# Splitting four products of a gate unit into high and low parts, and reordering vector work in an up-projection unit

## Chip, cores and metric

One core of a Trainium2 (trn2) chip runs the whole program. The metric is the device time of one execution in microseconds (us); the median of several runs counts.

## What is computed

One layer of a hybrid autoregressive decoder, for a prompt of 512 positions and 8 single-position samples that share the weights (520 columns in all), model width 2048, everything in fp32. The parts that matter here:

```python
def layer(x, ...):
    ...
    h2 = rmsnorm(x, g_ffn_pre)
    up, gt = jnp.split(h2 @ w_ffn_up, 2, axis=-1)          # 2048 -> 2 x 5632
    uc, new_ffn = causal_dwconv(up, prev_ffn, ffn_conv_w)
    f = (jax.nn.gelu(uc + ffn_conv_b, approximate=True) * gt) @ w_ffn_down
    x = x + rmsnorm(f, g_ffn_post)
    x = x + jax.nn.sigmoid(x @ w_ple_gate) * (p @ w_ple)   # w_ple_gate: 2048 -> 2048
```

The change lies in `h2 @ w_ffn_up` ("up") and in `x @ w_ple_gate` ("gate").

## The kernel before

**Units and products.** Each large matrix product is cut into units. A unit makes two tiles of 128 output features for all 520 positions. Operand and weights are seen as 2x2 blocks (upper and lower half of the contraction, left and right 260 columns), and a unit computes them by seven block products, numbered 0 to 6, in place of eight (a Strassen-Winograd scheme). For that it needs sums and differences of the operand blocks, made once for each set of units (`t1` to `t4`, lines 1947 to 1975), and of the weight blocks, made in each unit: `s1` (in these sets done by GpSimd's two DMAs, the second accumulating, lines 2573 to 2588), `s3` (L1921), `s2` (L1931) and `s4` (L1940). Product 1 reads the `s1` sum, product 2 the `s2` difference and `t2`, product 4 `s3` and `t3`, product 5 `s4`, product 6 `t4`. Every product has two halves of four contraction tiles each.

**Two ways to do a product.** A raw product (`raw_product`, L1023) multiplies fp32 tiles: 8 matmuls, which the profile shows as 16 records. A split product (`split_product`, L1058) takes a high and a low part of both factors and does three cheaper matmuls a tile, 24 in all: high x high, low x high, high x low. It needs the weight's high part `v_hi` (ScalarE, `v_high`, L1219), its low part `v_lo` (VectorE, `v_low`, L1889; four buffers for each, in turn), the operand's high part `o_hi` (ScalarE, `o_high`, L1246) and its low part `lo` (VectorE, `o_low`, L1987). The operand's parts are made once for a set, the weights' in each unit.

**Sets.** The seven sets of units (`SETS`) are: the input projection, w_o, up (set 2, 44 units, from `U_UP`), three for down, and gate (`S_GATE`, 8 units, from `U_GATE`). The first unit of sets 0, 2 and 6 is plain (`plain_unit`, L989): eight fp32 block products with no differences at all, since these are made meanwhile. The second unit of these three sets is done raw in all seven products (`in_fp32` says so); all later units are split. Sets 1, 3, 4 and 5 split products 0 to 4 of their second unit already (`early_split`).

**What sets the order.** Each engine runs its own list of instructions, in the order in which the program text emits it, and waits on semaphores. In gate, VectorE's list in `plain_unit` (L2056 to 2076) is `s3`, `t1`, `t2`, `t3`, `t4`, `o_low(0)`; then `second_unit` (L2078) emits slot by slot, for i from 0 to 13, evictions, `s2`, `s4`, `s3` of the next unit, the `o_low` that `lows` names, and `v_low`. In up it is `t1`, `s3`, `t2`, `t3`, `t4`, and in `second_unit` `s2` first, then `o_low` 0 to 4 in slots 1, 3, 5, 7, 9; `o_low(5)` comes at the unit's end and `o_low(6)` in slot 1 of the third unit. ScalarE's list in gate's `plain_unit` (L1289) is `o_high` 0 to 4 and then four copies out of PSUM (L1299); product 0 of the second unit waits for the first of these. `unit` (VectorE at L2106, ScalarE at L1322) is the list of an ordinary unit: `v_low` or `v_high` four halves ahead, slot by slot.

SyncE loads the weights (`load`), a quarter at a time, once the quarter's last reader is done; in gate its list between the second and the fourth unit also has the two stores of the first unit's output, and loads of `pl_sb` and `xx_sb`.

Of the kernel before, what the change touches and what calls it, by code (L numbers as in the profile page):

```python
# [26 lines left out]
U_UP = U_O + KD // 2  # L27
# [36 lines left out]
def h_of(u, j, h=0):  # L64
    return 14 * u + 2 * j + h + (2 * NBR if u >= U_O else 0) + (NPH if u >= U_UP else 0)
# [18 lines left out]
def build(nc, sstream, x_in, p_in, chan_in, sinkp_in, sinks_in, cstate_in, fstate_in,  # L84
# [5 lines left out]
    with ExitStack() as ctx:  # L90
# [173 lines left out]
        def set_of(u):  # L264

            return max(s for s, (u0, _, _) in enumerate(SETS) if u >= u0)

        def is_first(u):
            return u == SETS[set_of(u)][0]
# [8 lines left out]
        def is_second(u):  # L278
            return u > 0 and is_first(u - 1)
# [7 lines left out]
        def early_split(s):  # L287

            return s in (1, 3, 4, 5)

        def in_fp32(u, j):

            return is_first(u) or is_second(u) and (j >= 5 or not early_split(set_of(u)))

        def low_order(s):

            return (0, 3, 1, 5, 2, 4, 6) if s == S_GATE else (0, 1, 2, 3, 4, 5, 6)

        def summed(u):

# [21 lines left out]
        def s_of(u, j, h=0):  # L322
            return place[u, j, h]
# [36 lines left out]
        def of_form(s):  # L360

            return s if s < 3 else s - 3
# [811 lines left out]
        def _(act):  # L1174
# [114 lines left out]
            def plain_unit(s, d11, d12, d22, d21):  # L1289

                u = SETS[s][0]
                early = 1 if s == 2 else 5
                for j in range(early):
                    o_high(s, j)
                act.wait_ge(v_used, h_of(u, 6, 1) + 1)
                for dst, (a, b), done in ((d11, (0, 1), c11_out), (d12, (1, 1), c12_out),
                                          (d22, (1, 0), c22_out), (d21, (0, 0), c21_out)):
                    if dst is not None:
                        nc.scalar.activation(dst, pair[a][:, b, 0:HALF], ACT.Copy).then_inc(done, 1)  # L1299
                for j in range(early, 2 if s == 2 else 5):  # L1300
                    o_high(s, j)
# [20 lines left out]
            def unit(u, evac, ahead=14):  # L1322

                n = s_of(u, 0)
                for i in range(14):
                    if (u, i // 2, i % 2) in place and s_of(u, i // 2, i % 2) + 4 < n + ahead:
                        v_high(s_of(u, i // 2, i % 2) + 4)
                    evac(u, i)
                    if u == U_GATE + 2 and i == 2:
                        o_high(S_GATE, 6)  # L1330

            def by(s, evac, first=None, last=14):

                u0, n, _ = SETS[s]
                if early_split(s):
                    early_unit(s, first or evac)
                    unit(u0 + 1, evac, 18)
                else:
                    if u0 not in PLAIN:
                        first_unit(s, first or evac)  # L1340
                    second_unit(s, evac)
                for u in range(u0 + 2, u0 + n):
                    unit(u, evac, 16 if u == U_O - 1 else 18 if u == U_UP - 1 else 14 if u == u0 + n - 1 else 18)

# [309 lines left out]
        def _(dve):  # L1654
# [269 lines left out]
            def s2(u, h):  # L1924

                if u >= U_END:
                    return
                if in_fp32(u, 0):
                    dve.wait_ge(v_used, h_of(u, 0, h) + 1)
                sum_ready_1(dve, u, h)  # L1930
                dve.tensor_tensor(quarter(u, 0, h), w_src(u, 1, h), quarter(u, 0, h), ALU.subtract)\  # L1931
                   .then_inc(s2_done, 1)
# [44 lines left out]
            def o_low(s, j):  # L1977

                if s == S_GATE and j == 5:
                    slot_free(dve, s, 5)  # L1980
                for h in range(2):
                    if s < S_GATE or j not in (0, 3, 5):
                        u = SETS[s][0]
                        dve.wait_ge(v_used, h_of(u + 1 if in_fp32(u + 1, j) else u, j, h) + 1)
                    dve.wait_ge(o_hi_rdy, 14 * s + 2 * j + h + 1)
                    k = halves(s, h)
                    dve.tensor_tensor(lo_of(s, j)[:, k, :], raw_of(s, j)[:, k, :],  # L1987
                                      o_hi[j][:, k, :].bitcast(f32), ALU.subtract).then_inc(o_rdy, 1)

            def both_halves(f, *a):  # L1990
                f(*a, 0)
                f(*a, 1)
# [63 lines left out]
            def plain_unit(s):  # L2056

                u = SETS[s][0]
                if s == 2:
                    for k in range(KH):  # L2060
                        h2_row(k)
                    dve.wait_ge(h2_rdy, KH)
                    both_halves(t1, s)
                both_halves(s1, u + 1)
                both_halves(s3, u + 1)
                if s == 2:
                    for k in range(KH, KD):
                        h2_row(k)
                    dve.wait_ge(h2_rdy, KD)
                else:  # L2070
                    both_halves(t1, s)
                both_halves(t2, s)
                both_halves(t3, s)
                both_halves(t4, s)
                if s == S_GATE:
                    o_low(s, 0)

            def second_unit(s, evac):  # L2078

                u = SETS[s][0] + 1  # L2080
                nxt = s_of(u + 1, 0)
                lows = {1: 3, 3: 1, 4: 5, 5: 2, 9: 4} if s == S_GATE else {2 * j + 1: j for j in range(6)}
                if s == 2:
                    lows = {1: 0, 3: 1, 5: 2, 7: 3, 9: 4}
                for i in range(14):
                    if i < 13:
                        evac(u, i)
                    if i in (0, 1):
                        s2(u, i)
                    if i in (2, 3):  # L2090
                        s1(u + 1, i - 2)
                    if i in (6, 7):
                        s4(u, i - 6)
                    if i in (8, 9):
                        s3(u + 1, i - 8)
                    if i in lows:
                        o_low(s, lows[i])
                    if i >= 10:
                        v_low(nxt + i - 10)
                    if i in (11, 12):  # L2100
                        s2(u + 1, i - 11)
                evac(u, 13)
                if s == 2:
                    o_low(s, 5)

            def unit(u, evac, last):  # L2106

                n = s_of(u, 0)
                ahead = 16 if u == U_O - 1 else 14 if last and u != U_UP - 1 else 18
                adds = set_of(u) in (4, 5)  # L2110
                first = (1, 3, 5, 9) if adds else (9,)
                for i in range(14):
                    if i in first:
                        evac(u, i)
                    if (u, i // 2, i % 2) in place and s_of(u, i // 2, i % 2) + 4 < n + ahead:
                        v_low(s_of(u, i // 2, i % 2) + 4)
                    if is_second(u) and i == 1:
                        o_low(set_of(u), 4)
                    if is_second(u) and i == 13:
                        o_low(set_of(u), 5)  # L2120
                    if is_second(u - 1) and i == (5 if u > U_GATE else 1):
                        o_low(set_of(u), 6)
                    if i in (4, 5):
                        s4(u, i - 4)
                    if i in (8, 9) and u != U_O - 1 and u + 1 not in PLAIN:
                        s1(u + 1, i - 8)
                    if i in (10, 11) and u != U_O - 1 and u + 1 not in PLAIN:
                        s3(u + 1, i - 10)
                    if i in (12, 13) and not last:
                        s2(u + 1, i - 12)  # L2130
                    if i not in first:
                        evac(u, i)

            def by(s, evac, first=None):
                u0, n, _ = SETS[s]
                if early_split(s):
                    early_unit(s, first or evac)
                    unit(u0 + 1, evac, False)
                else:
                    if u0 in PLAIN:  # L2140
                        plain_unit(s)
                    else:
                        first_unit(s, first or evac)
                    second_unit(s, evac)
                for u in range(u0 + 2, u0 + n):
                    unit(u, evac, u == u0 + n - 1)

# [585 lines left out]
```

## Time and profile before

| | |
|---|---|
| median of 3 runs | 2707.23 us |
| lowest, highest | 2706.88, 2708.92 us |
| the profiled execution's own time | 2706.55 us |
| its span, first to last instruction | 2704.4 us |
| TensorE busy | 2683.6 us (99%) |
| VectorE busy | 2162.8 us (80%) |
| ScalarE busy | 1361.9 us (50%) |
| mean granted TensorE clock | 0.999 of 2.4 GHz |

The span is what the trace shows; 2.15 us of the execution lie around it. Busy shares are averages over stages, so the stretches of the two units have to be read by themselves. In a timeline a row is one instruction or several merged ones: start, time from first start to last end, engine, line, what it writes and reads, and in brackets the idle time of the engine before it with what ended it. TensorE names only the kernel's tiles: `pair` is PSUM. "issue" is a wait for which the profile shows no releaser.

### The profile page before, as it was taken

What the parts mean: (1) busy time and instruction counts of PE and PEld (TensorE: products, weight loads), DVE (VectorE), ACT (ScalarE), POOL (GpSimd) and SP (SyncE); (2) the same over time, 40 slices, a digit from 0 to 9 for tenths busy, and PEclk for the clock granted to TensorE, in tenths of its full rate; (3) what the DMA queues carried; (4) which work ended last, traced back from release to release, by engine and by line L of the source; (5) the groups of instructions that cost most, each with busy time, mean ns of one, the idle gap of its engine ahead of it and who ended that gap; (6) DMA issues with size and microseconds to landing.
All of it is one profiled execution on the core that took longest, in us unless ns stands there. A gap on an engine that the chain in (4) does not pass through costs nothing.

```text
span 2704.4 us, 55262 instructions
## 1 busy us (share of the span) xinstructions
PE 2683.6 (99%) x21029; PEld 2615.1 (97%) x21029; DVE 2162.8 (80%) x3845; ACT 1361.9 (50%) x2459; POOL 144.4 (5%) x214
## 2 busy tenths in 40 slices
PE   9999999999999999999999999999999999999999
PEld 8999999999999999979999999999999999999899
DVE  5988888777753587898888888888888768789887
ACT  5444455555542255645555555555555453445344
POOL 0000000000000000000000000000000000000000
PEclk9999999999999999999999999999999999999999
DMA  6333333333344455565566655666568575565674
GB/s 225 119 118 119 111 114 116 122 129 130 120 181 140 168 141 148 190 213 170 161 189 189 187 160 164 208 183 189 154 187 294 164 240 166 163 205 167 227 257 150
DMA packets 150356, 458.29 MB, mean 169 GB/s; under 512 B 15881, under 2 KB 46481, under 8 KB 146816
## 3 DMA queue, kind: packets, MB, share of 16 engines
q1 hardware_dynamic: 125184, 367.61, 38.1%
q0 software_dynamic: 24864, 88.52, 14.8%
q8 instruction: 81, 1.33, 0.2%
q14 instruction: 83, 0.68, 0.1%
q10 hardware_dynamic: 144, 0.15, 0.0%
HBM read 403.37 MB, written 54.11 MB: 169 GB/s over the span
## 4 chain that ended last, share of the span: by engine, by line
PE 97%; DVE 1%; issue 1%; ACT 0%; DMA 0%; SPq 0%; DVEq 0%; ACTq 0%
PE pair L1058 76%; PE pair L1023 7%; PE pair L1142 7%; PE pair L989 3%; PE pair L803 1%; PE pair L1112 1%; PE pair L871 1%; PE pair L894 1%; PE pair L885 1%; PE pair L819 0%; DVE v_lo L1889 0%; PE pair L955 0%; DMA s_raw<-in_sstream 0%; DVE nv_s L1676 0%; DVE lo L1987 0%
## 5 line engine op out<-in xcount | busy, mean ns | idle before, releaser
L1058 PE MATMUL pair<-o_hi,v_hi 128*128 128x260 f32 x5778 | 1639.5, 284 | 2.1 <-DVE v_lo L1889 1.9
L1058 PE MATMUL pair<-o_hi,v_lo 128*128 128x260 f32 x5778 | 1631.2, 282 | 0.0
L1219 ACT ACTIVATE v_hi<-s_raw 128x512 fp32r<-128x512 f32 (+1 forms) x1328 | 826.5, 626 | 1006.8 <-PE pair L1058 841.9
L1058 PE MATMUL pair<-lo,v_hi 128*128 128x260 f32 x4140 | 1170.2, 283 | 0.0
L1889 DVE TENSOR_TENSOR v_lo<-s_raw,v_hi 128x512 fp32r<-128x512 f32 (+1 forms) x1264 | 859.4, 682 | 341.6 <-ACT v_hi L1219 302.1
L1058 PEld LDWEIGHTS pair<-o_hi,v_hi 128*128 128x128 f32 x5778 | 1086.3, 188 | 15.8 <-issue 12.5
L1058 PEld LDWEIGHTS pair<-o_hi,v_lo 128*128 128x128 f32 x5778 | 1088.5, 188 | 0.0
L1058 PEld LDWEIGHTS pair<-lo,v_hi 128*128 128x128 f32 x4140 | 778.1, 188 | 0.4
L1058 PE MATMUL pair<-lo_E,v_hi 128*128 128x260 f32 x834 | 236.0, 283 | 0.0
L1058 PE MATMUL pair<-lo_A,v_hi 128*128 128x260 f32 x804 | 226.6, 282 | 0.0
L1219 ACT ACTIVATE v_hi<-s_one 128x512 fp32r<-128x512 f32 (+1 forms) x212 | 132.1, 626 | 178.2 <-PE pair L1058 153.3
L1931 DVE TENSOR_TENSOR s_raw<-s_one,s_raw 128x512 f32<-128x512 f32 (+1 forms) x226 | 151.9, 675 | 14.6 <-PE pair L1023 14.6
L1058 PEld LDWEIGHTS pair<-lo_E,v_hi 128*128 128x128 f32 x834 | 156.5, 188 | 0.1
L1940 DVE TENSOR_TENSOR s_raw<-s_raw,s_raw 128x512 f32<-128x512 f32 (+1 forms) x226 | 152.3, 675 | 0.0
L1921 DVE TENSOR_TENSOR s_raw<-s_raw,s_raw 128x512 f32<-128x512 f32 (+1 forms) x226 | 151.3, 675 | 0.0
L1058 PEld LDWEIGHTS pair<-lo_A,v_hi 128*128 128x128 f32 x804 | 151.1, 188 | 0.0
L1889 DVE TENSOR_TENSOR v_lo<-s_one,v_hi 128x512 fp32r<-128x512 f32 (+1 forms) x212 | 143.3, 678 | 5.2 <-ACT v_hi L1219 1.7
L1023 PE MATMUL pair<-raw,s_raw 128*128 128x260 f32 x628 | 141.1, 383 | 1.0 <-issue 0.5
L1023 PEld LDWEIGHTS pair<-raw,s_raw 128*128 128x128 f32 x628 | 118.5, 190 | 19.8 <-issue 0.9
L2586 POOL DMA_DIRECT2D s_one<-in_sstream x81 | 44.4, 548 | 1385.7 <-DVE s_raw L1931 1053.8
L1142 PE MATMUL pair<-br_hi,v_lo 128*128 128x260 f32 x512 | 103.2, 283 | 0.0
L1142 PE MATMUL pair<-br_lo,v_hi 128*128 128x260 f32 x512 | 103.0, 283 | 0.0
(229 smaller groups left out, 2358.6 us busy)
## 6 DMA issues: line engine op xcount, KB each, us to landing
s_raw<-in_sstream SPq DMA_DIRECT2D x468, 512.0 KB, 4.8
s_one<-in_sstream POOLq DMA_DIRECT2D x146, 512.0 KB, 5.2
raw<-f_scr SPq DMA_DIRECT2D x12, 1040.0 KB, 7.4
s_raw<-in_sstream SPq DMA_DIRECT2D x32, 384.0 KB, 4.0
g_scr<-d_h SPq DMA_DIRECT2D x16, 520.0 KB, 2.7
g_in<-g_scr SPq DMA_DIRECT2D x32, 260.0 KB, 2.7
x_scr<-y_sb SPq DMA_DIRECT2D x8, 1040.0 KB, 4.9
s_one<-in_sstream POOLq DMA_DIRECT2D x16, 384.0 KB, 4.7
```

Source lines behind the costliest of these rows:

```text
L803: mm = pe.matmul(pair[2 + n][:, h, 0:HALF], w[:, quarter_of(k)[2]], x_half(k, h), start=k == 0, stop=k == KD - 1, skip_group_check=True)
L871: mm = pe.matmul(bank[g][:, v * 256:(v + 1) * 256], q_blk[n % 2][HD * g:HD * g + HD, v, :], kT_sb[HD * g:HD * g + HD, blk * BLK:(blk + 2) ...
L989: mm = pe.matmul(pair[a][:, b, 0:HALF], s_raw[r % 2][q][:, k % KH * P:(k % KH + 1) * P], src, start=k == 0, stop=k == nk * 2 - 1, skip_gro ...
L1023: mm = pe.matmul(out, w[:, kk * P:kk * P + P], src[:, k, :], start=j in (0, 1, 3) and k == 0, stop=k == nk - 1, skip_group_check=True)
L1058: mm = pe.matmul(out, wt[:, slot, kk * P:kk * P + P], r[:, k, :], start=j in (0, 1, 3) and k == 0 and n == 0, stop=k == nk - 1 and n == 2, ...
L1142: mm = pe.matmul(pair[2 + p][:, half, 0:HALF], wt[:, slot, kk * P:kk * P + P], r[:, half * HALF:(half + 1) * HALF], start=k == 0 and i == ...
L1219: nc.scalar.activation(v_hi[:, n % 4, 0:width], src, ACT.Copy, scale=0.5 if u == "br" else 1.0).then_inc(v_hi_rdy, 1)
L1889: ins = dve.tensor_tensor(v_lo[:, n % 4, 0:width], src, high, ALU.subtract)
L1921: dve.tensor_tensor(quarter(u, 2, h), quarter(u, 0, h), quarter(u, 2, h), ALU.subtract)\
L1931: dve.tensor_tensor(quarter(u, 0, h), w_src(u, 1, h), quarter(u, 0, h), ALU.subtract)\
L1940: dve.tensor_tensor(quarter(u, 1, h), quarter(u, 1, h), quarter(u, 0, h), ALU.subtract)\
L2586: pool.dma_start(s_one[:, 0:n], sstream[r_of(u), 2, :, 0:n]).then_inc(s1_dma, 16)
```

## The change

Gate's second unit computes products 0 to 3 split and 4 to 6 raw. For it ScalarE makes four `v_hi` ahead of the four copies, and VectorE's list gets behind `t4`: `o_low(0)`, two `v_low`, `o_low(1)`, two `v_low`, `s2` of the second unit, `o_low(2)`, `o_low(3)`; the unit itself runs through the ordinary `unit`, with `o_low(5)` in slot 1 and `o_low(4)` in slot 11. In up, `s2` of the second unit is emitted ahead of `t3` and `t4`, `t4` behind `o_low(0)`, and `o_low` 5 and 6 in slots 2 and 5 of the third unit.

```diff
+        def first_raw(s):
+            return 4 if s == S_GATE else 5 if early_split(s) else 0
         def in_fp32(u, j):
-            return is_first(u) or is_second(u) and (j >= 5 or not early_split(set_of(u)))
+            return is_first(u) or is_second(u) and (j >= first_raw(set_of(u)))
         def low_order(s):
-            return (0, 3, 1, 5, 2, 4, 6) if s == S_GATE else (0, 1, 2, 3, 4, 5, 6)
+            return (0, 1, 2, 3, 5, 4, 6) if s == S_GATE else (0, 1, 2, 3, 4, 5, 6)
...
@@ scalar, plain_unit
                     o_high(s, j)
+                if s == S_GATE:
+                    for n in range(4):
+                        v_high(s_of(u + 1, 0) + n)
                 act.wait_ge(v_used, h_of(u, 6, 1) + 1)
...
@@ scalar, unit
                     evac(u, i)
+                    if u == U_GATE + 1 and i == 1:
+                        o_high(S_GATE, 5)
...
@@ scalar and vector, by
-                    second_unit(s, evac)
+                    if s == S_GATE:
+                        unit(u0 + 1, evac, ...)
+                    else:
+                        second_unit(s, evac)
...
@@ vector, o_low
-                    if s < S_GATE or j not in (0, 3, 5):
+                    if s == S_GATE and j in (1, 2):
+                        dve.wait_ge(t4_done, 2 * of_form(s) + 2)
+                    elif s < S_GATE or j not in (0, 3, 5):
...
@@ vector, plain_unit
                 both_halves(t2, s)
-                both_halves(t3, s)
-                both_halves(t4, s)
+                if s != 2:
+                    both_halves(t3, s)
+                    both_halves(t4, s)
                 if s == S_GATE:
+                    nxt = s_of(u + 1, 0)
                     o_low(s, 0)
+                    v_low(nxt)
+                    v_low(nxt + 1)
+                    o_low(s, 1)
+                    v_low(nxt + 2)
+                    v_low(nxt + 3)
+                    both_halves(s2, u + 1)
+                    o_low(s, 2)
+                    o_low(s, 3)
...
@@ vector, second_unit
-                    if i in (0, 1):
+                    if i in (0, 1) and s != 2:
                         s2(u, i)
+                    if i == 0 and s == 2:
+                        both_halves(s2, u)
+                        both_halves(t3, s)
+                    if i == 2 and s == 2:
+                        both_halves(t4, s)
...
                 evac(u, 13)
-                if s == 2:
-                    o_low(s, 5)
...
@@ vector, unit
                     if is_second(u) and i == 1:
-                        o_low(set_of(u), 4)
-                    if is_second(u) and i == 13:
-                        o_low(set_of(u), 5)
-                    if is_second(u - 1) and i == (5 if u > U_GATE else 1):
+                        o_low(set_of(u), 5 if u > U_GATE else 4)
+                    if is_second(u) and i == (11 if u > U_GATE else 13):
+                        o_low(set_of(u), 4 if u > U_GATE else 5)
+                    if u == U_UP + 2 and i in (2, 5):
+                        o_low(2, 5 + i // 5)
+                    elif is_second(u - 1) and u != U_UP + 2 and i == (5 if u > U_GATE else 1):
                         o_low(set_of(u), 6)
```

## Rows read from the trace of the kernel before

**Rows 1.** The page's first part: busy time, share of the span, instructions.

```profile
PE 2683.6 (99%) x21029; PEld 2615.1 (97%) x21029; DVE 2162.8 (80%) x3845; ACT 1361.9 (50%) x2459; POOL 144.4 (5%) x214
```

**Rows 2.** TensorE's waits: releaser, total us, times, longest.

```profile
PE pair L1023 <- issue: 6.1, 3, 4.3
PE pair L1058 <- DVE v_lo L1889: 1.9, 3, 1.2
```

**Rows 3.** Chain of waits, in order of time: start, us, what; up, then gate.

```profile
1181.28 4.30 issue
1185.58 19.46 PE pair L1023 x80
...
2523.14 28.29 PE pair L989 x128
2551.44 1.26 issue
2552.69 24.79 PE pair L1023 x112
2577.48 121.03 PE pair L1058 x1008
```

**Rows 4.** TensorE's timeline in up: second unit, then products 2 and 3 of the third.

```profile
1177.61 3.67 PE L1023 MATMUL pair<-raw,s_one 128*128 128x260 f32 x16
1185.58 5.43 PE L1023 MATMUL pair<-raw_E,s_raw 128*128 128x260 f32 x16 [4.30 <-issue]
...
1211.38 0.39 PE L1058 MATMUL pair<-o_hi,v_hi 128*128 128x260 f32 x1 [0.49 <-DVE v_lo L1889]
...
1215.76 0.39 PE L1058 MATMUL pair<-o_hi,v_hi 128*128 128x260 f32 x1 [1.24 <-DVE v_lo L1889]
```

**Rows 5.** Windows: stretch, length, TensorE busy, granted clock, DMA share, GB/s.

```profile
1185.60:1188.00 2.40, 2.40 (x8) 0.66 0.12 22
1188.00:1190.00 2.00, 2.00 (x7) 0.55 0.72 244
...
2553.00:2556.00 3.00, 3.00 (x15) 1.00 0.80 321
```

**Rows 6.** VectorE's timeline in up, second and third unit.

```profile
1177.88 2.39 DVE L1959 TENSOR_TENSOR raw_E<-raw 128x1040 f32<-128x1040 f32 x2
...
1184.80 1.29 DVE L1931 TENSOR_TENSOR s_raw<-s_one,s_raw 128x512 f32<-128x512 f32 x2
...
1190.61 0.69 DVE L2460 TENSOR_TENSOR fzb<-fzb,rstd 128x520 f32<-128x520 f32 x1
...
1193.53 0.69 DVE L1940 TENSOR_TENSOR s_raw<-s_raw,s_raw 128x512 f32<-128x512 f32 x1
...
1199.73 0.42 DVE L2157 TENSOR_TENSOR g_half<-pair,g_half 128x260 f32<-128x260 f32 x1
...
1205.33 0.68 DVE L1889 TENSOR_TENSOR v_lo<-s_raw,v_hi 128x512 fp32r<-128x512 f32 x1
...
1219.29 0.69 DVE L1889 TENSOR_TENSOR v_lo<-s_raw,v_hi 128x512 fp32r<-128x512 f32 x1
...
1224.01 0.69 DVE L1889 TENSOR_TENSOR v_lo<-s_raw,v_hi 128x512 fp32r<-128x512 f32 x1 [0.85 <-ACT v_hi L1219]
```

**Rows 7.** VectorE's timeline in gate, end of the plain unit and start of the second.

```profile
2542.69 2.39 DVE L1951 TENSOR_TENSOR raw<-y_sb 128x1040 f32<-128x1040 f32 x2
...
2551.91 2.39 DVE L1987 TENSOR_TENSOR lo<-y_sb,o_hi 128x1040 fp32r<-128x1040 f32 x2
```

**Rows 8.** ScalarE's timeline in gate, the same stretch and a little behind.

```profile
2552.23 1.19 ACT L1299 ACTIVATE d_first<-pair 128x260 f32<-128x260 f32 x4
...
2563.77 1.14 ACT L1219 ACTIVATE v_hi<-s_raw 128x512 fp32r<-128x512 f32 x2
```

**Rows 9.** Timelines of GpSimd's and SyncE's queues in gate.

```profile
2560.24 0.55 POOL L2586 DMA_DIRECT2D s_one<-in_sstream  x1 [51.74 <-PE pair L1023]
...
2576.42 0.33 SPq L736 DMA_DIRECT2D pl_sb<-ple_scr  x1
```

More of the change, by code:

```diff
@@ L1340, in by @@
                         first_unit(s, first or evac)
-                    second_unit(s, evac)
+                    if s == S_GATE:
+                        unit(u0 + 1, evac, 18)
+                    else:
+                        second_unit(s, evac)
                 for u in range(u0 + 2, u0 + n):
@@ L2081, in second_unit @@
                 nxt = s_of(u + 1, 0)
-                lows = {1: 3, 3: 1, 4: 5, 5: 2, 9: 4} if s == S_GATE else {2 * j + 1: j for j in range(6)}
+                lows = {2 * j + 1: j for j in range(6)}
                 if s == 2:
@@ L2143, in by @@
                         first_unit(s, first or evac)
-                    second_unit(s, evac)
+                    if s == S_GATE:
+                        unit(u0 + 1, evac, False)
+                    else:
+                        second_unit(s, evac)
                 for u in range(u0 + 2, u0 + n):
```

## The prediction

> **What bounds the kernel now.** The page's first part comes first: TensorE is busy for 2683.6 of 2704.4 us, VectorE for 80% [rows 1]. So only two things move the end: TensorE's own work, and its gaps. Its list of waits shows how few gaps there are [rows 2]; the chain of waits puts them in place [rows 3]. In up, one of 4.30 us stands ahead of product 2 of the second unit; in gate, one of 1.26 us ahead of product 0 of the second unit. Up's third unit has two more, 0.49 and 1.24 us, ahead of products 2 and 3 [rows 4]. The gap of 4.30 us has a tail: the product behind it took 5.43 us where the one ahead took 3.67, and the granted clock of that stretch was 0.66 and then 0.55, so near the lower of the two levels, 1.2 GHz against 2.4 [rows 4, 5]. The gap of 1.26 us had no such tail (clock 1.00) [rows 5].
>
> VectorE's timeline is then to be read, for it releases nearly all of this. In up it has no bracket, so no idle time, between 1177.88 and 1224.01 us [rows 6]. In gate it works without a break to the end of `o_low(0)` [rows 7]. The 80% of the page hides two stretches where VectorE is the bound.
>
> **Prices.** A raw product: 24.79 us for seven, 3.54 each. A split one: 1008 matmuls are 42 products of 24 in 121.03 us, 2.88 each [rows 3]. Splitting one saves 0.66 us, four save 2.6. On VectorE a pair of 128x1040 halves holds the queue for 2.30 us (2.39 from first start to last end, less the 0.09 by which neighbours overlap), a weight operation of 128x512 for 0.60 (pair 1.29) [rows 6]. ScalarE makes a pair of `v_hi` in 1.14 us [rows 8], so four in about 2.2.
>
> **Gate, step by step.** Up to `o_low(0)` nothing on VectorE moves; it starts at 2551.91 and holds the queue to 2554.21 [rows 7]. Behind it, at the prices above: two `v_low` to 2555.41, `o_low(1)` to 2557.71, two `v_low` to 2558.91, `s2` to 2560.11, `o_low(2)` to 2562.41, `o_low(3)` to 2564.71. Only then comes the ordinary unit, whose slots 0 and 1 make the first two `v_low` of product 2 (2564.71 and 2565.31); `o_low(5)` follows to 2568.21, and the `v_low` of product 3 at 2568.21 and 2568.81.
>
> TensorE's side:
> - Product 0 needs its first `v_low`, done 2554.21 + 0.69 = 2554.9, so it starts near 2554.95, not at 2552.69. The other thing it needs, the first copy, comes at the same time: ScalarE was free for the copies at 2552.23 [rows 8], now makes four `v_hi` first (2.2 us) and ends the first copy near 2554.7. The copies are hidden by 0.2 us, and would set the start if VectorE were earlier. Queued behind them are only later evictions.
> - Product 0 ends at 2557.83. Product 1 needs `v_low` at 2557.71, done 2558.4: gap 0.6. It ends at 2561.33.
> - Product 2 needs `v_low` done at 2565.4: gap 4.1. What is queued there is the low part of products 2 and 3, 4.6 us of work that stands ahead of a 0.6 us instruction. It ends at 2568.33.
> - Product 3 needs its `v_low` at 2568.9: gap 0.6. It ends at 2571.83, and 4 to 6 follow raw: 2571.8 + 3 x 3.54 = 2582.5. Product 5's `s4` is done at 2570.6 and 2571.8 (slots 4 and 5), `o_low(4)` at 2579.2, well ahead of the third unit.
>
> Before, the unit ended at 2577.48 [rows 3]. So gate loses 5.0 us: 2.3 later at the start, 5.3 of gaps, 2.6 saved. Seen otherwise, before the raw products needed no `v_low` and no low part, and hid this VectorE work; the split ones wait for it. The new waits of `o_low(1)` and `o_low(2)` on `t4` cost nothing, `t4` being done at 2551.9 on the same engine. GpSimd's loads of the next weight sum now wait for `s2` at 2560.1, against product 1 and 2560.24 before [rows 9]: no move. SyncE's stores and `pl_sb` load wait for the end of `gate_add(0)`, which stands in slot 11 behind `o_low(4)` (2579.2), `s3` and the eviction of product 5 and so ends near 2580.6; the load leaves near 2581 instead of 2576.42 [rows 9], as late as the whole unit, and `gate_mul` of the third unit asks for it as much later. From the third unit on TensorE is the bound as before.
>
> **The clock in gate.** A gap of 4.1 us is nearest to the one of 4.30, which cost 5.43 - 3.67 = 1.76 us; one of 3.5 (2551.44 to 2554.95) lies between. If product 0 runs slow, the gap ahead of product 2 swallows it. If product 2 runs slow, the gap of 0.6 ahead of product 3 takes a third, and 1.1 us stay. Bounds: 0 (no fall, as after 1.26 us) and 1.8 (the slow stretch lies on product 3 and after). I take 1.1, from the nearer row. The Trainium skill, TensorE: Matmul & The Clock Gate, Part 1, says that the chip watches TensorE in step with its own time, not with the kernel's, so that the same kernel turns slow or fast at other places from run to run; by it this term would come and go between runs, 0 or 1.1, and the total with it. No row here shows two runs of one gap.
>
> **Up, step by step.** `s2` leaves its place at 1184.80 and runs behind `t2`, at 1180.18 [rows 6]. Product 2 is due at 1181.1 (1177.61 + 3.5), its weights are done at 1180.9 and 1181.5: the gap of 4.30 us and the slow product go, 6.06 us in all. But no VectorE work goes: `t3`, `o_low(0)`, `t4`, `o_low(1)` fill 1181.4 to 1190.6, and from L2460 at 1190.61 the list is as it was, with the same times [rows 6]. So TensorE runs ahead and waits:
> - products 2, 3, 4 end near 1191.65. Product 5 needs the first `s4`, 1193.53 + 0.69 = 1194.2: gap 2.6, end 1197.8.
> - product 6 needs the PSUM bank that L2157 clears, 1199.73 + 0.42 = 1200.15: gap 2.4, end 1203.7. Before: 1185.58 + 19.46 = 1205.04 [rows 3].
> - third unit: its second half waits for `v_low` at 1205.33 + 0.68 = 1206.0, gap 0.9. Products 1 to 4 then run through to 1219.0, since `o_low(5)` and `o_low(6)` have moved behind the `v_low` that gave the gaps of 0.49 and 1.24 [rows 4]. Product 5 needs the `v_low` at 1219.29, which has both `o_low` ahead of it before and after, done 1219.98: gap 0.9. With 5 and 6 the unit ends at 1225.8.
>
> Before, product 3 began at 1215.76, four products make 1227.3. So up gives 1.5 us of the 6 to 8 us that its gaps are worth. Bounds: 0, if the clock falls in the last two products, behind the new gaps, where nothing swallows it; 2.4, if VectorE frees 0.9 us ahead of product 5. The value taken is what the chain gives.
>
> **The sum.** Against the profiled execution, 2706.55 us (span 2704.4 and 2.15 around it): + 5.0 + 1.1 - 1.5 = + 4.6, or 2711.2. The median of the runs shown is 0.7 higher, so 2711.8 us.
>
> **The rivals.**
> - *Slower by over 0.2%.* Up gives nothing. Place: products 5 and 6 of up's third unit. After gaps of 2.6, 2.4, 0.9 and 0.9 us the clock falls there, for 1.8 us, and VectorE's lead is gone. It decides once the slow stretch starts after product 4. Price + 1.5: 2713.3. For it: a gap did bring the clock down here. Against it: these are shorter, and work lies between them.
> - *Faster.* TensorE's gaps alone count, and VectorE keeps pace: gate saves 2.6 us, up 6.06, so 2707.2 - 8.7 = 2698.5. It would need VectorE idle in both stretches; no bracket shows that [rows 6, 7].
> - *The change doesn't do what it says in gate:* the `v_low` of product 2 are not held up by two low parts. Then product 2 follows product 1, the gap of 4.1 and the clock term go, gate ends even (5.0 - 4.1 = 0.9), and the total is 2707.2 + 0.9 - 1.5 = 2706.6. The emitted order speaks against it.
> - *No fall of the clock* is within the forecast: 2710.7.
>
> **How the numbers follow.** A measurement of this kernel can tell about 0.2%, 5.4 us, from no change: 2701.8 to 2712.6. Chances: forecast 0.65 (with or without the clock term, 2710.7 to 2712.5), slower rival 0.15, gate even 0.13, faster 0.07. The forecast lies 0.8 us under the upper mark, so 0.15 of its 0.65 go over it (a slow stretch on product 3, up giving under 1 us). That makes slower 0.30, within 0.2% 0.63, faster 0.07. The range leaves out the faster rival and part of the even one: 2707 to 2714.5.
>
> **What the changed profile would show.** Right: in gate's second unit gaps ahead of products 0 (3.5), 1, 2 (4.1) and 3, with `v_lo` as the releaser, L1023 x48 for products 4 to 6, and the unit's end near 2582.5 less what up gave; in up no gap ahead of product 2, but ones ahead of 5 (`s4`, L1940) and 6 (L2157), and the third unit's end near 1225.8. Wrong: product 2 of gate within 1 us behind product 1; VectorE idle in up before 1219; a third unit of gate that waits for `pl_sb`; or a clock below 1.00 in up's third unit.

## The result, and the profile after

| | before | changed |
|---|---|---|
| median of 20 runs | 2707.28 us | 2711.10 us |
| lowest to highest | 2706.30 to 2708.92 | 2710.27 to 2712.78 |
| the profiled execution's own time | 2706.55 | 2711.78 |
| its span | 2704.4 | 2710.0 |

The ratio of changed to before is 1.0015 (95% interval 1.0009 to 1.0022): 3.8 us slower, less than the 0.2% that the prediction took as its mark, though the interval leaves out 1. The profiled execution of the changed kernel lies 0.7 us above its median.

TensorE's list of waits (releaser, total us, times, longest) has taken on five waits for `v_lo` in place of three [rows 2]:

```profile
PE pair L1062 <- DVE v_lo L1901: 8.6, 5, 3.9
PE pair L1027 <- DVE s_raw L1952: 2.6, 1, 2.6
PE pair L1027 <- DVE g_half L2189: 1.9, 1, 1.9
...
PE pair L1062 <- DVE f_low L2456: 0.9, 1, 0.9
```

TensorE's timeline in gate's second unit (start, us, line, operands, idle time before and what ended it) puts the largest in place; the raw product at 2572.39 is product 4:

```profile
2521.98 28.29 PE L993 MATMUL pair<-y_sb,s_raw 128*128 128x260 f32 x128 [1.04 <-DVE y_sb L2378]
2553.88 0.36 PE L1062 MATMUL pair<-o_hi,v_hi 128*128 128x260 f32 x1 [3.60 <-DVE v_lo L1901]
2557.39 0.36 PE L1062 MATMUL pair<-o_hi,v_hi 128*128 128x260 f32 x1 [0.41 <-DVE v_lo L1901]
2564.40 0.56 PE L1062 MATMUL pair<-o_hi,v_hi 128*128 128x260 f32 x1 [3.90 <-DVE v_lo L1901]
...
2572.39 3.67 PE L1027 MATMUL pair<-raw,s_raw 128*128 128x260 f32 x16
```

Gaps of 3.60, 0.41 and 3.90 us, where 3.5, 0.6 and 4.1 were worked out. A split product behind a wait lasts 3.10 us to the end of its last matmul in these rows (2553.88 to 2556.98), where one of many back to back takes 2.88, so a gap in the rows reads some 0.2 us shorter than in the prediction's chain. The starts can be compared as they are: products 0, 1 and 2 began 31.9, 35.4 and 42.4 us after the plain unit did, and 31.8, 35.3 and 42.3 were worked out. VectorE's timeline of the same stretch shows what stood ahead: its list without a pause, and two low parts (L2001, `lo_A` and `lo`) between `s2` (L1943) and the `v_lo` of product 2:

```profile
2557.75 1.29 DVE L1943 TENSOR_TENSOR s_raw<-s_one,s_raw 128x512 f32<-128x512 f32 x2
2558.96 2.39 DVE L2001 TENSOR_TENSOR lo_A<-raw,o_hi 128x1040 fp32r<-128x1040 f32 x2
2561.26 2.39 DVE L2001 TENSOR_TENSOR lo<-y_sb,o_hi 128x1040 fp32r<-128x1040 f32 x2
2563.56 1.29 DVE L1901 TENSOR_TENSOR v_lo<-s_raw,v_hi 128x512 fp32r<-128x512 f32 x2
```

The windows (stretch, length, TensorE busy, granted clock, DMA share, GB/s) show the clock near its lower level, 1.2 GHz, from inside the gap until past 2568:

```profile
2560.00:2562.00 2.00, 0.50 (x5) 1.00 0.50 100
2562.00:2564.00 2.00, 0.00 (x0) 0.61 0.41 162
2564.00:2566.00 2.00, 1.60 (x7) 0.50 0.33 39
2566.00:2568.00 2.00, 2.00 (x11) 0.50 1.02 188
2568.00:2570.00 2.00, 2.00 (x14) 0.69 0.22 43
```

The chain of waits gives the stage's end, to be held against [rows 3]; 8.16 us are products 2 and 3, 10.52 products 4 to 6:

```profile
2564.40 8.16 PE pair L1062 x48
2572.56 10.52 PE pair L1027 x48
2583.08 121.04 PE pair L1062 x1008
```

Executions differ by about 1 us in when a stage begins, so stages are measured from an anchor of their own. Up: from the start of its second unit's product 0 to the start of down. Before 1174.03 to 2054.37, 880.34 us; changed 1174.57 to 2053.22, 878.65. Up gained 1.7 us. Gate: from the start of the plain unit to the start of the third. Before 2523.14 to 2577.48, 54.34 us; changed 2521.98 to 2583.08, 61.10. Gate lost 6.8 us in this execution.

Up's second unit in the changed kernel, TensorE's timeline:

```profile
1181.66 3.67 PE L1027 MATMUL pair<-raw_E,s_raw 128*128 128x260 f32 x16
...
1194.90 3.75 PE L1027 MATMUL pair<-raw,s_raw 128*128 128x260 f32 x16 [2.56 <-DVE s_raw L1952]
1200.53 3.77 PE L1027 MATMUL pair<-raw,s_raw 128*128 128x260 f32 x16 [1.88 <-DVE g_half L2189]
1205.19 0.38 PE L1062 MATMUL pair<-o_hi,v_hi 128*128 128x260 f32 x1 [0.89 <-DVE f_low L2456]
1220.36 0.39 PE L1062 MATMUL pair<-o_hi,v_hi 128*128 128x260 f32 x1 [0.51 <-DVE v_lo L1901]
```

The gap of 4.30 us and the slow product behind it [rows 4] are gone; gaps of 2.56, 1.88, 0.89 and 0.51 us stand ahead of products 5 and 6 and in the third unit.

### The profile page after: what moved, and what is told of

It is laid out like the page before. It is cut to its first block, busy times and chain, and to the rows that moved or that the text cites. A ratio compares the mean times of both kernels' runs of the same rounds, so it can differ in the third digit from the quotient of the medians.

```text
span 2710.0 us, 55352 instructions
## 1 busy us (share of the span) xinstructions
PE 2682.4 (99%) x21061; PEld 2615.7 (97%) x21061; DVE 2167.7 (80%) x3853; ACT 1365.5 (50%) x2467; POOL 144.5 (5%) x214
## 4 chain that ended last, share of the span: by engine, by line
PE 95%; DVE 3%; issue 1%; ACT 0%; DMA 0%; SPq 0%; DVEq 0%; ACTq 0%
PE pair L1062 76%; PE pair L1146 7%; PE pair L1027 6%; PE pair L993 2%; PE pair L807 1%; PE pair L1116 1%; PE pair L875 1%; PE pair L898 1%; DVE v_lo L1901 1%; PE pair L889 1%; DVE lo L2001 1%; DVE y_sb L2372 0%; DVE y_sb L2378 0%; PE pair L823 0%; DMA s_raw<-in_sstream 0%
## 5 line engine op out<-in xcount | busy, mean ns | idle before, releaser
L1943 DVE TENSOR_TENSOR s_raw<-s_one,s_raw 128x512 f32<-128x512 f32 (+1 forms) x226 | 152.2, 677 | 13.1 <-PE pair L1027 13.1
```

## The experiments

All medians below are of 11 runs, beside 27 or 33 runs of the kernel before on the same chip (medians 2707.29, 2707.03 and 2707.03 us). A ratio's interval is some 0.1% to either side, 2 to 3 us, so single comparisons with before leave much open. The stages in the traces repeat to 0.05 us from run to run where the clock does the same, and carry the finer readings; but each trace shows one execution.

**The two parts by themselves.** `e1_up_only` is the kernel before with the hunks in up (`t3`, `t4`, `s2`, `o_low` 5 and 6); `e2_gate_only` the changed kernel without them.

> The kernel before with the changes in up alone; gate as before. My theory (VectorE is the bound through up's second and third unit, so only what the chain of its list allows comes back): 1.5 us less than before, about 2705.8 us; no gap ahead of product 2 of up's second unit, new ones of 2.6 and about 2 us ahead of products 5 and 6, third unit's end 1.5 us earlier relative to the start of the second unit. Rival (TensorE's gaps count for what they are): 6 us less, about 2701. Rival (up gives nothing): 2707.3.

> The changed kernel with up put back; gate as changed. My theory (the two parts simply add): 1.5 us above the changed kernel's 2711.1, so about 2712.6 us, 5.3 above before; gaps in gate's second unit of 3.5, 0.5, 4 and 0 to 0.6 us. Rival (up gave nothing and gate lost only 3.8): 2711.1.

Up alone: 2704.93 us (2704.56 to 2705.26; ratio 0.9992, 0.9983 to 1.0001). Gate alone: 2712.35 us (2711.30 to 2714.04; ratio 1.0021, 1.0012 to 1.0030). In the traces up takes 878.64 us in the first and 880.30 in the second (880.34 before), so neither part moves the other's stage. The medians add less well: 2.4 us less and 5.1 more make 2.7 more, and 3.8 was measured. The 1.1 us between lies within the intervals; part of it can be the clock, which the next runs bear on. In gate alone TensorE's timeline reads:

```profile
2555.12 0.56 PE L1062 MATMUL pair<-o_hi,v_hi 128*128 128x260 f32 x1 [3.60 <-DVE v_lo L1901]
2565.64 0.36 PE L1062 MATMUL pair<-o_hi,v_hi 128*128 128x260 f32 x1 [1.77 <-DVE v_lo L1901]
2569.15 0.36 PE L1062 MATMUL pair<-o_hi,v_hi 128*128 128x260 f32 x1 [0.40 <-DVE v_lo L1901]
...
2572.13 3.67 PE L1027 MATMUL pair<-raw,s_raw 128*128 128x260 f32 x16
```

Here the clock fell behind the first gap (0.56 in the window 2554 to 2558), not the later one. The slow products 0 and 1 ran into the wait ahead of product 2, which shrank from 3.90 to 1.77 us, and the second unit ended 5.2 us late (59.58 us after the plain unit began, against 54.34), not 6.8: the same text of gate, another place of the slow clock, 1.5 us less.

**Filling the gaps.** To take the clock out of it, seven idle-bank matmuls ahead of products 0 and 2:

```diff
                 for j in range(7):
+                    if s == S_GATE and j in (0, 2):
+                        for n in range(7):
+                            pe.matmul(pair[3][:, n % 2, 0:HALF], ones[:, :], chan[:, 0:HALF],
+                                      start=True, stop=True)
```

> The changed kernel with 14 matmuls of no use in gate, seven into an unused bank ahead of product 0 and seven ahead of product 2 of the second unit; each seven take about 3.2 us, less than the gap they stand in. The result isn't touched. If the higher half of the changed kernel's runs (2711.3 to 2712.8 against 2710.3 to 2710.9) comes from a clock that falls after the gap of 3.9 us: clock 1.00 throughout, products 2 and 3 in 5.8 to 6.4 us together instead of 8.2, no run above 2711.0, median near 2710.6. If the spread has another cause: median stays at 2711.1 with runs up to 2712.5. If the gaps were not gaps of waiting: 6 us slower.

2710.14 us (2709.54 to 2710.66). TensorE's timeline and chain:

```profile
2564.03 0.36 PE L1066 MATMUL pair<-o_hi,v_hi 128*128 128x260 f32 x1 [0.84 <-DVE v_lo L1905]
2567.54 0.36 PE L1066 MATMUL pair<-o_hi,v_hi 128*128 128x260 f32 x1 [0.39 <-DVE v_lo L1905]
...
2570.65 10.52 PE pair L1027 x48
2581.17 121.01 PE pair L1066 x1008
```

The clock stayed at 1.00 in gate, the second unit ended 5.2 us late (2521.61 to 2581.17, 59.56 us), and no run lies above 2710.66, where the changed kernel reached 2712.78. The kernel does more work and is 1.0 us faster by the medians (the kernel before took 2707.29 us beside it and 2707.28 beside the changed kernel). So gate loses 5.2 us with the clock left out, and the clock adds to it by run: nothing in e2's trace, 1.5 us in the changed kernel's. More than 1.5 is likely in some runs, since the changed kernel's highest lies 2.6 us above e3's median; no trace shows such a run. Up alone and gate's 5.2 us, 2704.93 + 5.2 = 2710.1, make the time measured for e3.

**The order of the low parts.** Same work in gate, with the two `v_low` of product 2 ahead of `o_low(3)`, and `o_low(5)` two slots later:

```diff
                     o_low(s, 2)
+                    v_low(nxt + 4)
+                    v_low(nxt + 5)
                     o_low(s, 3)
...
-                    if (u, i // 2, i % 2) in place and s_of(u, i // 2, i % 2) + 4 < n + ahead:
+                    if (u != U_GATE + 1 or i > 1) and (u, i // 2, i % 2) in place \
+                            and s_of(u, i // 2, i % 2) + 4 < n + ahead:
                         v_low(s_of(u, i // 2, i % 2) + 4)
-                    if is_second(u) and i == 1:
+                    if is_second(u) and i == (3 if u > U_GATE else 1):
                         o_low(set_of(u), 5 if u > U_GATE else 4)
```

> The changed kernel, with VectorE's two v_low of product 2 put ahead of o_low(3), and o_low(5) moved from slot 1 to slot 3 behind the v_low of product 3. Same work, another order. My theory (gate's loss is low parts standing ahead of the v_low that TensorE waits for): the gap ahead of product 2 falls from 3.9 to 1.8 us, the one ahead of product 3 stays at 0.6, gate's second unit ends 2.3 us earlier than with a full clock in the changed kernel, and with no fall of the clock there the total is about 2708.4 us. Rival (the loss is VectorE's whole work, whatever its order): 2711.1, the gap only moves to a later product.

2708.94 us (2708.39 to 2709.53). The wait ahead of product 2 fell to 0.70 us (product 0 ran slow in this trace, with a clock of 0.57 from 2554 to 2558, and took the rest), and the second unit ended 2.9 us late instead of 5.2 (2521.60 to 2578.87, 57.27 us). The order was 2.3 us of the loss. But the third unit lost 1.1 us again. Its chain of waits:

```profile
2578.87 2.88 PE pair L1062 x24
2582.26 12.22 DMA s_raw<-in_sstream
2595.08 1.37 issue
2597.01 104.00 PE pair L1062 x864
```

A load of the fourth unit's weights was 12.2 us under way and VectorE, which waits for it in slot 8, stood 1.37 us with evictions behind; TensorE then waited 0.86 us for one of them. In SyncE's list it follows two output stores that wait for `gate_add`. So `gate_add` was moved ahead, the one edit over e4:

```diff
-                    muls, adds = ((6, 7), (10, 11)) if u == U_GATE + 1 else ((1, 2), (3, 6))
+                    muls, adds = ((6, 7), (8, 9)) if u == U_GATE + 1 else ((1, 2), (3, 6))
```

> The reordered gate of e4 with gate_add of the first unit's tiles in slots 8 and 9 in place of 10 and 11, ahead of o_low(4). In e4 VectorE stood 1.37 us in gate's third unit, with the weights of the fourth in the chain of waits, 12.2 us under way. Theory: SyncE's list holds these loads behind two output stores that wait for gate_add; earlier adds let them go 3 to 4 us earlier and that wait goes, 0.9 to 1.1 us less than e4, about 2707.9 us. Rival (the loads are slow by themselves, or the wait is for something else): as e4, 2708.9.

2707.70 us (2707.28 to 2708.02), 1.2 less than e4. SyncE's loads leave at 2577.20 instead of 2580.65, and from the third unit on the chain has no wait (2578.88, 121.00 us). The four loads left 3.5 us earlier and also landed sooner, a median of 9.3 us after issue against 10.6 in e4; most of the difference is when they left. This new bound stood right behind the one removed.

**Which half of the change in up gained.** The chain worked out for the prediction, done again for each half, said that all of it came from `o_low` 5 and 6, though the larger gap was removed by the other half.

`e5_up_order` is the kernel before with only this:

```diff
-                both_halves(t3, s)
-                both_halves(t4, s)
+                if s != 2:
+                    both_halves(t3, s)
+                    both_halves(t4, s)
...
-                    if i in (0, 1):
+                    if i in (0, 1) and s != 2:
                         s2(u, i)
+                    if i == 0 and s == 2:
+                        both_halves(s2, u)
+                        both_halves(t3, s)
+                    if i == 2 and s == 2:
+                        both_halves(t4, s)
```

and `e6_up_lows` with only this:

```diff
                 evac(u, 13)
-                if s == 2:
-                    o_low(s, 5)
...
-                    if is_second(u - 1) and i == (5 if u > U_GATE else 1):
+                    if u == U_UP + 2 and i in (2, 5):
+                        o_low(2, 5 + i // 5)
+                    elif is_second(u - 1) and u != U_UP + 2 and i == (5 if u > U_GATE else 1):
                         o_low(set_of(u), 6)
```

> The kernel before with only the first half of the change in up: s2 ahead of t3 and t4 in the second unit; o_low(5) and o_low(6) stay where they were. My theory, the chain of VectorE's list: the gap of 4.30 us ahead of product 2 goes, gaps ahead of products 5 and 6 and of the third unit take its place, and the third unit's gaps of 0.5 and 1.2 us ahead of products 2 and 3 stay, set by the same v_low as before: 0.0 us, about 2707.3. Rival (the removed gap and its slow clock are what up gained): 1.5 us less or more, 2705.8 or below.

> The kernel before with only the second half of the change in up: o_low(5) and o_low(6) in slots 2 and 5 of the third unit; s2 stays behind t3 and t4. My theory: the gap of 4.30 us ahead of product 2 of the second unit stays, slow clock included, the gaps of 0.5 and 1.2 us in the third unit go, one of 0.5 to 0.8 us ahead of its product 5 comes, and the whole gain of up is there: 1.5 us less, about 2705.8. Rival (the gain came from s2): 2707.3.

e5: 2706.21 us (2705.65 to 2706.92), e6: 2705.94 us (2704.95 to 2706.64); by medians they can't be told apart, and e5's lies between the 2707.3 of its theory and the 2705.8 of its rival. By the traces they can. e5, TensorE: 1173.40 to 2053.54, 880.14 us, 0.2 gained; the gap of 1.24 us is still there:

```profile
1180.49 3.67 PE L1023 MATMUL pair<-raw_E,s_raw 128*128 128x260 f32 x16
...
1193.72 3.74 PE L1023 MATMUL pair<-raw,s_raw 128*128 128x260 f32 x16 [2.55 <-DVE s_raw L1940]
1199.35 5.46 PE L1023 MATMUL pair<-raw,s_raw 128*128 128x260 f32 x16 [1.89 <-DVE g_half L2163]
...
1214.90 0.39 PE L1058 MATMUL pair<-o_hi,v_hi 128*128 128x260 f32 x1 [1.24 <-DVE v_lo L1889]
```

e6: 1175.02 to 2053.86, 878.84 us, 1.5 gained, with the large gap in place:

```profile
1186.56 5.43 PE L1023 MATMUL pair<-raw_E,s_raw 128*128 128x260 f32 x16 [4.29 <-issue]
...
1221.01 0.39 PE L1058 MATMUL pair<-o_hi,v_hi 128*128 128x260 f32 x1 [0.51 <-DVE v_lo L1889]
```

That leaves e5's median 0.8 us under before and its stage 0.2. In e5's trace product 6 ran slow, behind its gap of 1.89 us: 5.46 us, with a clock of 0.50 from 1201 to 1203. The stage didn't end later for it, for the gap of 1.24 us behind is still there. Since the removed gap is where the clock falls, the kernel before got nine filler matmuls in it (the edit of e3, with `s == 2 and j == 2`):

> The kernel before with nine matmuls of no use, into an unused bank, ahead of product 2 of up's second unit; they take about 4 us and stand in the gap of 4.30 us. The result isn't touched. Open is why the kernel with the change in up alone gained 2.4 us in its median where its trace shows 1.7, and why the runs of before spread over 2.6 us and its own over 0.7. If it is the clock after the gap of 4.30 us, which in some runs falls or lasts where nothing swallows it: median about 2706.5 us, runs within about 1 us, no run above 2707.3, clock 1.00 in up. If the spread comes from elsewhere: median 2707.1 and runs up to 2708.3 as before.

2706.44 us; ten runs from 2705.87 to 2707.01 and one at 2707.85, against 2706.11 to 2708.69 beside it. The clock was 1.00 through up and the stage took 880.12 us, as good as the 880.14 of e5: the 0.2 us is there with the gap filled too, so it is the price of the slow product, and the gap itself was worth nothing. Median and spread went as expected of the clock, the one run above 2707.3 did not. The clock behind the gap of 4.30 us is thus likely to have cost the kernel before some 0.4 us in the median beyond what its profiled execution shows; its trace is of an execution below its median, so where the clock fell in the longer ones stays open.

**A gate that hides its low parts.** If the loss is low parts on the path, a split with fewer of them ahead should gain. `e7_gate03` splits only products 0 and 3. ScalarE's four `v_hi` come behind `o_high(0)`, the copies behind `o_high(2)`. The edit over the changed kernel, cut to the choice of products and VectorE's list:

```diff
-            return is_first(u) or is_second(u) and (j >= first_raw(set_of(u)))
+            return is_first(u) or is_second(u) and (j not in (0, 3) if set_of(u) == S_GATE
+                                                  else j >= first_raw(set_of(u)))
...
                     both_halves(t1, s)
-                both_halves(t2, s)
-                if s != 2:
-                    both_halves(t3, s)
-                    both_halves(t4, s)
                 if s == S_GATE:
                     nxt = s_of(u + 1, 0)
                     o_low(s, 0)
                     v_low(nxt)
                     v_low(nxt + 1)
-                    o_low(s, 1)
-                    v_low(nxt + 2)
-                    v_low(nxt + 3)
+                both_halves(t2, s)
+                if s != 2:
+                    both_halves(t3, s)
+                if s == S_GATE:
                     both_halves(s2, u + 1)
-                    o_low(s, 2)
                     o_low(s, 3)
+                    v_low(nxt + 2)
+                    v_low(nxt + 3)
+                if s != 2:
+                    both_halves(t4, s)
...
+                    if is_second(u) and u > U_GATE and i in (1, 3, 10, 11):
+                        o_low(S_GATE, {1: 5, 3: 1, 10: 2, 11: 4}[i])
```

> The change in up, and in gate another split: only products 0 and 3 of the second unit split, 1, 2, 4, 5, 6 raw. ScalarE makes the four v_hi behind o_high(0), and copies out of PSUM behind o_high(2); VectorE's list is t1, o_low(0), two v_low, t2, t3, s2, o_low(3), two v_low, t4, and the others' low parts inside the unit. If low parts on the path are gate's loss and raw products hide them, then product 0 starts 0.5 us after the plain unit (no gap of 3.5), no gap above 0.3 us follows, and the second unit ends 1.8 us before where it ended in the kernel before: 2707.3 - 1.5 - 1.8 = 2704.0 us. Rival (any split product in this unit makes VectorE the bound): gaps ahead of product 3 or 6 and 2705.8 or more.

2708.26 us (2707.54 to 2712.07): a miss of 4 us. Its trace is of a longer execution, 2710.82 us. The second unit did end some 1 us early in it, but gaps of 0.81, 0.62 and 3.20 us in the third followed, the last behind an eviction that waited for the fourth unit's weights, as in e4, and with a slow clock behind it (0.68 from 2596 to 2600). `e10_gate03_adds` lets the loads go earlier and moves evictions ahead of low parts, over e7:

```diff
+                    if u == U_GATE + 1 and i == 9:
+                        v_low(s_of(u + 1, 1))
+                        v_low(s_of(u + 1, 1, 1))
-                    if (u, i // 2, i % 2) in place and s_of(u, i // 2, i % 2) + 4 < n + ahead:
+                    if (u != U_GATE + 1 or i < 6) and (u, i // 2, i % 2) in place \
+                            and s_of(u, i // 2, i % 2) + 4 < n + ahead:
                         v_low(s_of(u, i // 2, i % 2) + 4)
-                    if is_second(u) and u > U_GATE and i in (1, 3, 10, 11):
-                        o_low(S_GATE, {1: 5, 3: 1, 10: 2, 11: 4}[i])
+                    if is_second(u) and u > U_GATE and i in (1, 3, 10, 13):
+                        o_low(S_GATE, {1: 5, 3: 1, 10: 2, 13: 4}[i])
...
-                    muls, adds = ((6, 7), (10, 11)) if u == U_GATE + 1 else ((1, 2), (3, 6))
+                    muls, adds = ((6, 7), (8, 9)) if u == U_GATE + 1 else ((1, 2), (3, 6))
```

> e7 (only products 0 and 3 split) with gate_add in slots 8 and 9, the third unit's v_low of product 1 behind the copies of slot 9, o_low(4) in slot 13. Theory: e7's second unit did end 1.1 us earlier than before's, and the 5.6 us it then lost were the weights of the fourth unit arriving late (3.2 us) and evictions behind low parts (0.8, 0.6), with a slow clock behind the gap of 3.2; with loads earlier and evictions first, the second unit ends 1.2 to 1.6 us before where it ended in the kernel before and nothing is lost behind: 2704.9 (up alone) - 1.2 to 1.6 = about 2703.5 us. Rival (splitting two products costs VectorE as much as TensorE saves): 2704.9 or more.

2703.52 us (2703.15 to 2703.94; ratio 0.9986, 0.9977 to 0.9995): faster than before, than the changed kernel by 7.6 us, and than up alone by 1.4. Its chain of waits in gate:

```profile
2521.89 28.29 PE pair L994 x128
2550.18 0.93 issue
2551.11 3.11 PE pair L1063 x24
2554.22 7.01 PE pair L1028 x32
2561.23 2.87 PE pair L1063 x24
2564.11 10.52 PE pair L1028 x48
2574.63 121.08 PE pair L1063 x1008
```

The plain unit to the third takes 52.74 us, 1.6 less than before, with one gap of 0.93 us (a copy behind `o_high(2)`). The edit's three parts weren't run one by one, so how much each gave stays open.

## Why the prediction was right, step by step

The forecast was 2711.8 us, the median is 2711.1. The three terms came to + 5.2 (traces), + 1.0 and - 2.4 (medians), where + 5.0, + 1.1 and - 1.5 were forecast. By its terms:

- *Gate, + 5.0.* Held: 5.2 us in e2 and e3. The start (2.3 later), the starts of products 1 and 2 and the releaser are those of the chain of VectorE's list. e4 shows the named cause: two instructions moved ahead of `o_low(3)` give 2.3 us back.
- *The clock in gate, + 1.1, between 0 and 1.8.* The right mechanism, but not a constant of the kernel. It was 1.5 in the profiled run of the changed kernel (6.8 - 5.2), and 0 in e2, where the wait ahead of product 2 took it. Between the changed kernel's median and that of e3 it makes 1.0, so that 1.1 came out so close is in part luck. The text named both outcomes, and said which gap would swallow a slow product 0; it did. What it had too small is the slow stretch, priced at 1.8 us at most from one raw product: products 0 and 1 together took 6.62 us in the changed kernel (2553.88 to 2560.50, with the gap of 0.41 in it) and 8.75 in e2 (2555.12 to 2563.87), 2.1 us more. The fall came at product 2 in the changed kernel's trace, and at product 0 in those of e2, e4 and e9. What the Trainium skill says there of the clock (TensorE: Matmul & The Clock Gate, Part 1), that the chip's watching isn't in step with the kernel, fits this; no two traces of one kernel were taken that could show it.
- *Up, - 1.5.* The trace gives 1.7, the halves 0.2 and 1.5. Mis-sized is the median's share: 2.4 us for up alone. The sum was made against one execution, and the kernel before likely loses some more to the clock in others (e8: 0.4 us; the rest stays open). The gap of 4.30 us with its slow product, 6.06 us in all, was worth 0.2; the chain, done again for e5, had it at nothing.
- *Two releasers.* The third unit of up waited 0.89 us for the eviction L2456 (1204.62 to 1205.05), at its first product, where the text had a `v_low` for its second half: about the same time, another name. The gap ahead of its product 5 is 0.51, not 0.9. In gate product 3 came without a gap, since product 2 ran slow.
- *The rivals.* "Up gives nothing" is out: 878.6 us in each of the seven traces with the whole change in up. In five of them (e3, e4, e7, e9, e10) the clock did fall at product 5 there, which took 5.43 us, as this rival asked; but the wait ahead of product 6 shrank from 1.9 to 0.2 and the stage's end didn't move. The prediction held that nothing there would swallow a slow product, though its own chain had a gap of 2.4 us ahead of product 6. The rival's price of 1.5 us, and the lower bound of 0 for up, thus had no ground for a slow product 5; a slow product 6 was seen in e5 alone, and cost nothing there. "Faster" needed VectorE idle; it wasn't. "Gate even" needed product 2 right behind product 1; there were 3.9 us.
- *The signs of being wrong* stayed away: the clock was 1.00 from 1204 to 1226 in up's third unit, VectorE was busy for 47.9 of the 48 us from 1178 to 1226, and gate's third unit ran without a wait.
- *SyncE's loads,* costed at nothing since they moved with the unit, were right for this change (VectorE waits 0.28 us there, and TensorE works from 2583.08 without a wait). Their cover was thin: e4, which only sped up the second unit, lost 1.1 us to them.

## What to carry to other kernels

On an in-order engine that is the bound, work only changes places: in the traces, removing the largest gap of TensorE was worth 0.2 of 6 us, while moving two late-needed low parts behind early-needed work was worth 1.5 (by the medians, which can't be told apart, 0.8 and 1.1). A cheaper product is dearer if its preparation stands on the path: put what is needed next first, count the preparations against the time until their product is due, and split those products whose preparation has cover. Once a stage is quicker, follow the loads for the stage after next through the queue that issues them, down to the store they stand behind.

## What the runs showed of the hardware

- A fall of TensorE's clock isn't in itself a loss. Behind a gap of 2.55 us it slowed a product by 1.7 us (5.43 against 3.75) in five of seven traces of up and not in the other two, and the next wait took all of it. In an eighth (e5) the product behind the gap of 2.55 ran at full clock, and the one behind the next, of 1.89, took 5.46 us. It cost 1.5 us in the changed kernel's gate, where no wait behind it was long enough.
- It can fall at either of two gaps of the same text of gate: behind the one of 3.90 us in the changed kernel's trace, behind the one of 3.60 in e2's, e4's and e9's. It makes most of the spread: 2.5 us over 20 runs without fillers, 1.1 over 11 with them (e3).
- Useless matmuls in a gap, shorter than it, took 1.0 us off the changed kernel's median, and no cost of them shows.
- A weight load of 512 KB takes a median of 4.8 us to land over the whole kernel before. The four of gate's fourth unit, beside stores and other loads (DMA share 1.03 from 2582 to 2600 in e4, 368 GB/s), took 9.4 us before, 10.5 in the changed kernel, 10.6 in e4 and 9.3 in e9: it is mostly a matter of the stretch, and by some 1 us one of when they leave.
